# Hyena convolution spread between the query/key/value matmuls, attention spread between gate and projection tiles

## The chip, the cores and the metric

The kernel runs on one core of one Trainium2 chip. The metric is the device time of one execution in microseconds (us). All data are float32. In the trace a float32 matmul leaves two records, so a group "x128" is 64 matmuls; a transpose leaves one.

## The reference, cut to what matters

One trunk layer runs on 128 context tokens and 256 latent tokens (384 rows in all, width 2048).

```
mod  = silu(cond) @ w_ada + b_ada             # shift, scale, gate, twice
h    = rms_norm(x) * (1 + scale1) + shift1
proj = h @ w_in      # q 2048 | k 512 | v 512 | hyena 3 x 1024 | gate_attn 2048 | gate_hy 2048
y_attn = attention(rope(rms_norm(q)), rope(rms_norm(k)) + cache, v + cache) @ w_attn_o
u    = short_conv(hyena part) -> x0, x1, vh
y_hy = (x0 * long_conv(vh * x1, filter)) @ w_hy_o        # long_conv: product of spectra
m    = (sigmoid(gate_attn) * y_attn + sigmoid(gate_hy) * y_hy) @ w_out
x    = x + gate1 * rms_norm(m)
x    = x + gate2 * rms_norm(expert_choice_ffn(modulate(rms_norm(x))))     # 16 experts
```

There are 16 query heads and 4 key/value heads of width 128. The outputs are both streams and the context keys and values.

## The kernel before

Weights stream through `ring`, four slots of 2 MB. SyncE's queue loads them with `turn` (L262), four blocks a turn, each of 1024 rows by 512 columns (runs of 2 KB), and a block waits until the block four places ahead of it has been counted in `blocks_used` by TensorE. The order of all work is written out by hand for each engine; the engines meet at counting semaphores. The stages, with what TensorE runs in each:

- **Start** (to about 132 us): modulation columns (`ada`, L342, and `ada_cols`, L351), the Hyena filter and its spectrum.
- **Hyena projection**: six turns of `ada`, `channels` and `ada_cols`. `channels` (L365) computes four output tiles of 128 channels by 384 tokens in four PSUM banks, with the contraction outermost: all four tiles end together. ScalarE (L835) and VectorE (L1190) then empty the banks through the short convolution; the next turn's `channels` waits for each bank (`conv_free`).
- **Hyena long convolution**: transposes (`u_tokens`, L460), forward spectra (`u_spectrum`, L470 and L473), products of spectra on VectorE (L1219 to L1227), `inverse` (L486, L488), and VectorE's gating (L1233, L1236). Nothing else is interleaved.
- **Query, key, value**: six turns of `ada`, `tokens` (L376: three banks of 128 tokens by 512 columns, contraction outermost) and `ada_cols`. ScalarE empties the banks (L859), VectorE normalises and rotates (`qk_norm`, L1251 to L1277) with a power on GpSimd (L1017).
- **Attention**, one head after another, software-pipelined by two heads: `queries` (L540), `scores` (L547 to L549), VectorE's maxima (L1298 to L1302), ScalarE's exponentials (L885), VectorE's `normalise` (L1307, L1310), transposes of the probabilities (L557, L559), their copies (L893, L1316), and the product with the values (L567, L569), copied by ScalarE (L897). GpSimd stages queries and values (L1026, L1031).
- **Gates and projections**: 32 gate tiles (`channels` on `hT`, ScalarE's Sigmoid, L924 and L929), then the attention projection (16 tiles, `channels` on `oT`), whose tiles VectorE multiplies with the gate (L1337, L1343), then the Hyena projection (16 tiles of half the depth, L613; VectorE L1349 to L1351).
- **Output projection**: `tokens` for four blocks of 512 columns, with `broadcast_gates` (L625) in the first two. ScalarE squares and copies each bank (L938, L940), VectorE scales (L1382); then the norm and the residual.
- **Routing and experts** (from about 1641 us): expert weights stream in pieces of 1 MB (L311, L317).

Two lines set which tile ends when, in `channels` and in `tokens`:

```
for k in range(HK):
    for c in range(4):          # tokens: for m in range(MT)
```

Of the kernel before, what the change touches and what calls it, by code (L numbers as in the profile page):

```python
# [23 lines left out]
P = 128  # L24
# [47 lines left out]
def build(nc, x_prompt, x_sample, cache_k, cache_v, cols, w_ada, w_in, qk_g, w_attn_o, f1_w, f_vec, f2_w,  # L72
# [3 lines left out]
    with ctx:  # L76
# [23 lines left out]
        ring = view(ring_t, 0, 4, HK, NC_)  # L100
        pieces = view(ring_t, 0, 8, 2 * FF)
# [11 lines left out]
        rope_t = view(RA, 0, 2, 2, HD)  # L113
        rot = view(RA, 512, 2, 2, 2, HD)
        gain_b = view(RA, 1536, 2, HD)
        t_a, t_b = view(RA, 1792, NC_), view(RA, 2304, NC_)
        kT = view(RA, 0, NKV, T + PAST)
        q_st = view(RA, 2048, 2, MT, HD)
        qT = view(RA, 2816, 2, T)
        v_st = view(RA, 3584, 4, HD)  # L120
# [11 lines left out]
        oT = view(RC, 0, NH, T)  # L132
        mix = view(RC, 0, MT, D)
# [12 lines left out]
        qkN = view(RE, 0, MT, D + KVW)  # L146
        vN = view(RE, 7680, 4, KVW)
        kcN = view(RE, 9728, KVW)
        prob = view(RE, 10240, 2, 2 * 384 + TC)
        sg = view(RE, 0, 2 * KT, T)  # L150
# [6 lines left out]
        yhT = view(RF, 0, HYT, T)  # L157
# [9 lines left out]
        probT = view(RG, 1024, 896)  # L167
# [25 lines left out]
        U_BANK = ((4, 5, 0), (1, 2, 3))  # L193
        Z_BANK = ((4, 0, 2), (0, 2, 4))

        def bank(b, n=512, off=0, p0=0, p1=P):
# [4 lines left out]
        blocks_used = sem("blocks_used")  # L201

# [15 lines left out]
        q_staged, v_staged, at_trk, at_kT, at_trq, at_qT, at_s, at_max, at_exp, at_norm, at_trp, at_pa, at_pb, at_o, at_oc = (  # L218
            sem(n) for n in ("q_staged", "v_staged", "at_trk", "at_kT", "at_trq", "at_qT", "at_s", "at_max", "at_exp", "at_norm",
                             "at_trp", "at_pa", "at_pb", "at_o", "at_oc"))  # L220
        mod2_read, gate_sig, ao_done, ho_done, mod3_read = (
            sem(n) for n in ("mod2_read", "gate_sig", "ao_done", "ho_done", "mod3_read"))
# [17 lines left out]
        B_QKV = B_HY + 6  # L240
        B_GA = B_QKV + 6
        B_GB = B_GA + 4
        B_AO = B_GB + 2
        B_HO = B_AO + 2
        B_WO = B_HO + 1
        B_EX = B_WO + 2

        def block(w, h, c):

            return w[h * HK * P:(h + 1) * HK * P, ds(c * NC_, NC_)].rearrange("(k p) n -> p k n", p=P)  # L250

# [4 lines left out]
        def _(sp):  # L256
# [17 lines left out]
            for base, ada0, in0, n in ((B_HY, 8, 6, 6), (B_QKV, 14, 0, 6), (B_GA, 20, 12, 4)):  # L274
# [57 lines left out]
        def _(pe):  # L332
            mm, trp = nc.tensor.matmul, nc.tensor.transpose

            def ada(b, j0, rows_bank):


                for h in range(2):
# [1298 lines left out]
```

## Time and profile before

| What | us |
|---|---|
| Median of three runs (2710.15 to 2712.53) | 2712.01 |
| The profiled execution | 2710.64 |
| Its span, first to last instruction | 2708.8 |
| TensorE busy in the span | 2429.6 |
| VectorE, ScalarE, GpSimd busy | 508.5, 237.4, 56.0 |

The profiled execution is 1.8 us longer than its span. The views used are: the page (busy time of each engine, and the span in 40 equal slices of 67.7 us), busy time by stretch, the chain of work that ended last, the timeline of single instructions, the groups of instructions, and the DMA issues.

### The profile page before, as it was taken

The page shows a single profiled execution, that of the slowest core. Times are in us where ns is not written, and L with a number is a line of the kernel's source. Part 1 is how long each engine was busy: PE and PEld are TensorE (multiplying, and loading weights), DVE is VectorE, ACT ScalarE, POOL GpSimd, SP SyncE. Part 2 cuts the span into 40 slices and gives each one's busy share as a digit, 9 for nine tenths or more (in the row PEclk, how much of TensorE's full clock was granted, in tenths as well). Part 3 has the DMA queues.
Part 4 walks back from the last instruction along what each step waited for, and adds up shares of the span by engine and source line. Part 5 has one row for each costly group of instructions (what it writes and reads, how often), then busy time and mean ns, then how long its engine had stood idle before and what let it go on. Part 6 is the DMA issues. An engine that isn't in the chain of part 4 may idle for free.

```text
span 2708.8 us, 23285 instructions
## 1 busy us (share of the span) xinstructions
PE 2429.6 (90%) x9040; PEld 1126.0 (42%) x9040; DVE 508.5 (19%) x1008; ACT 237.4 (9%) x485; POOL 56.0 (2%) x74
## 2 busy tenths in 40 slices
PE   6899997999978999999999995988888888888886
PEld 2355554444455555555554442422222222222222
DVE  4200116112152000000011114311111112111125
ACT  1100000000052100000000002200000000000001
POOL 0000000000010000000000000010000000000000
PEclk8899999999999999999999997999999999999998
DMA  9954541545413542222222231499999999999994
GB/s 350 372 190 154 214 155 50 184 162 207 155 39 140 202 170 95 93 93 93 93 100 87 93 114 41 194 421 422 422 422 422 422 422 422 422 422 422 422 420 195
DMA packets 172048, 644.46 MB, mean 238 GB/s; under 512 B 8423, under 2 KB 8840, under 8 KB 122536
## 3 DMA queue, kind: packets, MB, share of 16 engines
q1 hardware_dynamic: 169736, 635.55, 59.7%
q10 hardware_dynamic: 2208, 8.24, 0.8%
q8 instruction: 27, 0.44, 0.1%
q0 software_dynamic: 64, 0.13, 0.0%
q14 instruction: 13, 0.11, 0.0%
HBM read 640.21 MB, written 3.67 MB: 238 GB/s over the span
## 4 chain that ended last, share of the span: by engine, by line
PE 65%; DMA 18%; issue 8%; DVE 5%; DVEq 2%; ACT 1%; SPq 1%; ACTq 0%; POOL 0%; POOLq 0%
PE PS L365 21%; DMA ring<-in_w_up 16%; PE PS L376 15%; PE PS L773 8%; PE PS L728 6%; PE PS L613 3%; PE PS L342 2%; PE PS L698 2%; DMA ring<-in_w_ada 2%; PE PS L673 1%; DVE RG L1480 1%; DMA ring<-in_w_in 1%; PE PS L421 1%; DVE RE L1310 1%; PE PS L625 1%
## 5 line engine op out<-in xcount | busy, mean ns | idle before, releaser
L365 PE MATMUL PS<-RB,ring 128*128 128x384 f32 x1792 | 585.5, 488 | 10.5 <-DVE RE L1190 4.4
L728 PE MATMUL PS<-ring,RF 128*48 128x512 f32 x1920 | 434.9, 595 | 87.4 <-DMA ring<-in_w_up 85.6
L365 PEld LDWEIGHTS PS<-RB,ring 128*128 128x128 f32 x1792 | 339.4, 190 | 259.2 <-issue 17.9
L728 PEld LDWEIGHTS PS<-ring,RF 128*48 128x48 f32 x1920 | 135.8, 123 | 382.1 <-issue 381.4
L1475 DVE TENSOR_TENSOR RC<-RC,PS 128x512 f32<-128x512 f32 x192 | 122.5, 683 | 740.9 <-PE PS L698 740.9
L376 PE MATMUL PS<-ring,RB 128*128 128x512 f32 x576 | 248.8, 593 | 0.0
L773 PE MATMUL PS<-ring,RF 128*48 128x512 f32 x960 | 225.2, 630 | 0.0
L365 PE MATMUL PS<-RC,ring 128*128 128x384 f32 x512 | 169.6, 494 | 8.7 <-DVE RE L1343 6.6
L376 PE MATMUL PS<-ring,RE 128*128 128x512 f32 x384 | 168.7, 601 | 5.7 <-DVE RE L1351 5.7
L376 PEld LDWEIGHTS PS<-ring,RB 128*128 128x128 f32 x576 | 108.9, 190 | 139.9 <-issue 139.9
L773 PEld LDWEIGHTS PS<-ring,RF 128*48 128x48 f32 x960 | 63.2, 130 | 165.9 <-issue 165.6
L365 PEld LDWEIGHTS PS<-RC,ring 128*128 128x128 f32 x512 | 98.6, 193 | 79.7 <-issue 8.8
L698 PE MATMUL PS<-RG,RF 48*128 48x512 f32 x384 | 114.9, 675 | 2.1 <-ACT RG L985 1.3
L376 PEld LDWEIGHTS PS<-ring,RE 128*128 128x128 f32 x384 | 74.0, 193 | 99.6 <-issue 93.3
L342 PE MATMUL PS<-ring,RG 128*32 128x512 f32 x768 | 93.9, 631 | 13.3 <-DMA ring<-in_w_ada 10.9
L613 PE MATMUL PS<-RF,ring 128*128 128x384 f32 x256 | 82.8, 486 | 2.2 <-DVE RE L1343 2.2
L1190 DVE SCALAR_TENSOR_TENSOR RE<-PS,KC,RE 128x127 f32 (+1 forms) x96 | 33.9, 410 | 256.0 <-ACT RE L835 251.7
L979 ACT ACTIVATE RF<-PS 48x512 f32<-48x512 f32 x32 | 18.9, 592 | 606.1 <-PE PS L728 553.4
L613 PEld LDWEIGHTS PS<-RF,ring 128*128 128x128 f32 x256 | 48.6, 190 | 36.4 <-DVE RE L1343 2.8
L985 ACT ACTIVATE RG<-PS 48x512 f32<-48x512 f32 x64 | 37.9, 593 | 274.0 <-PE PS L773 252.9
L698 PEld LDWEIGHTS PS<-RG,RF 48*128 48x128 f32 x384 | 33.6, 194 | 63.8 <-issue 57.9
L342 PEld LDWEIGHTS PS<-ring,RG 128*32 128x32 f32 x768 | 23.0, 113 | 69.0 <-issue 52.5
(213 smaller groups left out, 1175.5 us busy)
## 6 DMA issues: line engine op xcount, KB each, us to landing
ring<-in_w_gate SPq DMA_DIRECT2D x128, 1024.0 KB, 13.2
ring<-in_w_up SPq DMA_DIRECT2D x128, 1024.0 KB, 14.3
ring<-in_w_down SPq DMA_DIRECT2D x128, 1024.0 KB, 13.5
ring<-in_w_ada SPq DMA_DIRECT2D x48, 2048.0 KB, 14.2
ring<-in_w_in SPq DMA_DIRECT2D x40, 2048.0 KB, 7.8
ring<-in_w_attn_o SPq DMA_DIRECT2D x8, 2048.0 KB, 7.9
ring<-in_w_out SPq DMA_DIRECT2D x8, 2048.0 KB, 7.9
ring<-in_w_hy_o SPq DMA_DIRECT2D x4, 2048.0 KB, 8.0
```

The costliest lines, as they stand in the source:

```text
L342: last = mm(bank(rows_bank, p0=32 * g, p1=32 * g + 32), condS[:, kk, :], ring[:, j0 + h, k, :], start=kk < 4, stop=kk >= KT - 4)
L365: last = mm(bank(b0 + c, T), ring[:, j0 + h, k, c * P:(c + 1) * P], rhs[:, h * HK + k, :], start=(h == 0 and k == 0), stop=(h == 1 and k = ...
L376: last = mm(bank(b0 + m), lhs[:, h * HK + k, m * P:(m + 1) * P], ring[:, j0 + h, k, :], start=(h == 0 and k == 0), stop=(h == 1 and k == H ...
L421: mm(bank(n % 4), arg[0:HF, m * P:(m + 1) * P], f3[0:HF, c * NC_:(c + 1) * NC_], start=True, stop=True).then_inc(f_tapmm, 1)
L613: last = mm(bank(4 * (c % 2) + j, T), ring[:, c, k, j * P:(j + 1) * P], yhT[:, k, :], start=k == 0, stop=k == HYT - 1)
L625: mm(bank(b0 + n % 2), one, diag[:, n % 2, :], start=True, stop=True).then_inc(done, 1)
L698: mm(bank(4 + n % 4), s_cur[64 * u:64 * u + SLOTS, m * P:(m + 1) * P], ye[64 * u:64 * u + SLOTS, i, :], start=True, stop=True).then_inc(e_ ...
L728: last = mm(bank(n, p0=64 * u, p1=64 * u + SLOTS), xeT[:, kk, 0, :] if first else x_cur[:, kk, :], pieces[:, (2 * i + u) % 8, k * FF + n * ...
L773: last = mm(bank(2 + i, p0=64 * u, p1=64 * u + SLOTS), hTe[:, k, :], pieces[:, k, (2 * i + u) * NC_:(2 * i + u + 1) * NC_], start=k == 0, ...
L985: last = A(ye[64 * u:64 * u + SLOTS, i, :], bank(2 + i, p0=64 * u, p1=64 * u + SLOTS), ACT.Copy)
L1190: last = stt(out=hyT[:, ds(i * 4 + j, 1), a:b].rearrange("p o t -> p (o t)"), in0=bank(j, b - a, a + o), scalar=w, in1=hyT[:, ds(i * 4 + j ...
L1475: tt(facc[:, m, q], facc[:, m, q], bank(4 + n % 4), ALU.add).then_inc(e_acc, 1)
```

## The change

It does the following.

- **Order inside a block.** `channels` and `tokens` now run the contraction innermost, so that tiles end one after another; each has its own semaphore (`hy_tile`, `qkv_tile`, `wo_tile`) and is emptied while the next runs.
- **Hyena convolution.** `tokens` calls `beside_qkv` after each group of eight matmuls (36 such slots in the six turns). Slots 0 to 19 hold the Hyena work, slots 24 to 28 the transposes of the keys, slot 34 the first query. The order of the turns is key, value, then the four query blocks. The spectra use banks 3 and 4 for every product, the inverse bank 5.
- **Attention** runs one head per turn, between the 16 Hyena gate tiles and the 16 Hyena projection tiles. The two-head pipeline, the second query, score and probability buffers and GpSimd's staging go.
- **Gates.** A gate tile is 16 matmuls (`gate`), followed by its projection tile, and VectorE merges both at once (`merge`). Sigmoid becomes (1 + tanh(x/2))/2: ScalarE runs Tanh with scale 0.5, VectorE adds 1 and multiplies, and the factor 1/2 moves into the gains (`times` 0.5) and the mean square (0.25).
- **Weights.** Gate and attention projection blocks are now 2048 rows by 256 columns (`wide`, runs of 1 KB, 2 MB each); SyncE's loops are written out.
- **Small DMAs.** The rotary table and the query/key gains are loaded right after the filter's DFT table instead of after the Hyena products.

```diff
-                    for k in range(HK):
-                        for c in range(4):
-                            if free and h == 0 and k == 0:
-                                pe.wait_ge(conv_free, free(c))
+                    for c in range(4):
+                        if h == 0:
+                            pe.wait_ge(conv_free, i * 4 + (c + 1))
+                        for k in range(HK):
...
-            def tokens(b, j0, b0, lhs, then=None):
+            def tokens(n, b0, lhs, free, free_at, done, then):
...
+                    for m in range(MT):
+                        if h == 0:
+                            pe.wait_ge(free, free_at(m))
+                        for k in range(HK):
...
+                        then(h, m)
...
+            def beside_qkv(p):
...
+                elif p == 3:
+                    pe.wait_ge(u_cp, 3)
+                    u_spectrum(0, 0)
...
+                elif p == 5:
+                    pe.wait_ge(z_ready, 1)
+                    u_spectrum(0, 1)
...
+                elif p < 13:
+                    inverse(p - 9)
+                elif p < 16:
+                    pe.wait_ge(z_ready, p - 10)
+                    u_spectrum(1, p - 13)
+                elif p == 16:
+                    pe.wait_ge(z_ready, 6)
+                    inverse(4)
...
+            pe.wait_ge(qkv_raw, 18)
+            for t in range(KT):
+                n, j = N_GH + 3 * (t // 4), t % 4
+                if t > 0:
+                    attend(t - 1)
+                scores(t)
+                gate(n + j // 2, t)
+                probabilities(t)
+                if t < KT - 1:
+                    queries(t + 1)
+                block_in(n + 2)
+                if t > 0:
+                    pe.wait_ge(mixed, t)
+                for k in range(HYT):
+                    last = mm(bank(F1, T), ring[:, (n + 2) % 4, k, j * P:(j + 1) * P], hyT[:, k, :],
+                              start=k == 0, stop=k == HYT - 1)
+                last.then_inc(blocks_used if j == 3 else proj_tile, 1)
+            attend(NH - 1)
             pe.wait_ge(at_oc, NH)
+            for t in range(KT):
+                n, j = N_GA + 6 * (t // 4), t % 4
+                if j == 0:
+                    ada(0, n % 4, 7, n)
+                gate(n + 2 + j // 2 * 2, KT + t)
+                pa = n + 3 + j // 2 * 2
+                block_in(pa)
+                pe.wait_ge(mixed, KT + t)
+                for k in range(NH):
+                    last = mm(bank(F1, T), wide[:, pa % 4, k, j % 2 * P:(j % 2 + 1) * P],
...
+                if j == 3:
+                    ada_cols(20 + t // 4, 0)
+            pe.wait_ge(mixed, 2 * KT)
...
             act.dma_start(dft_t, dft).then_inc(dft_in, 16)
+            act.dma_start(rope_t[:, :, :, :], rope).then_inc(qk_in, 16)
...
+            for t in range(KT):
+                if t > 0:
+                    head_out(t - 1)
+                exponentials(t)
+                half_tanh(N_GH + 3 * (t // 4) + t % 4 // 2, t)
+                act.wait_ge(at_trp, t + 1)
+                A(probT[:, 0:512], bank(B_P[0]), ACT.Copy).then_inc(at_pa, 1)
+                if t < KT - 1:
+                    query_copy(t + 1)
...
+            product(0, 0)
+            product(0, 1)
+            dve.wait_ge(qk_in, 32)
+            gained_rope(1)
+            qk_norm(0, 0)
+            product(0, 2)
+            gained_rope(0)
+            for n in range(4):
+                hyena_out(n)
+            for j in range(3):
+                product(1, j)
+            for n in range(4, 8):
+                hyena_out(n)
+            qk_norm(1, 6)
+            qk_norm(2, 9)
+            qk_norm(3, 12)
...
+            for t in range(KT):
+                maxima(t)
+                normalise(t)
+                if t == 1:
+                    qk_squares(4, 15)
+                elif 2 <= t < 5:
+                    qk_rotate(4, t - 2)
+                if t == 4:
+                    qk_ready()
+                dve.wait_ge(at_trp, t + 1)
+                V.tensor_copy(probT[:, 512:896], bank(B_P[1], 384)).then_inc(at_pb, 1)
+                merge(t)
```

## Rows read from the trace of the kernel before

**Rows 1.** The page's 40 slices: busy tenths of TensorE and of the DMA engines.

```profile
PE   6899997999978999999999995988888888888886
...
DMA  9954541545413542222222231499999999999994
```

**Rows 2.** Stretches: length, PE, PEld, DVE, ACT, POOL busy, PEclk, DMA share, GB/s.

```profile
744.00:842.00 98.00, 74.55 (x406) 57.19 (x410) 53.66 (x150) 51.09 (x150) 11.92 (x20) 0.98 0.08 27
411.00:469.00 58.00, 41.71 (x162) 27.71 (x161) 40.44 (x69) 5.01 (x10) 0.00 (x0) 0.91 0.13 44
...
60.00:140.00 80.00, 69.02 (x342) 27.49 (x341) 23.69 (x48) 7.78 (x13) 0.00 (x0) 0.86 0.99 362
```

**Rows 3.** The chain that ended last, in order of time: start, us, what.

```profile
323.48 39.63 PE PS L365 x122
...
370.75 39.63 PE PS L365 x122
...
473.03 41.40 PE PS L376 x96
...
518.82 41.40 PE PS L376 x96
...
845.44 41.48 PE PS L365 x128
```

**Rows 4.** Timeline, Hyena convolution: start, us, engine, line, shape [idle before].

```profile
435.62 1.89 PE L488 MATMUL PS<-RC 128*128 128x256 f32 x8
...
437.79 1.89 PE L488 MATMUL PS<-RC 128*128 128x256 f32 x8
...
443.30 0.69 DVE L1219 TENSOR_TENSOR RC<-PS,RA 128x512 f32<-128x512 f32 x1
...
446.80 0.69 DVE L1227 TENSOR_TENSOR RC<-RC,RG 128x512 f32<-128x512 f32 x1
...
469.39 3.20 PE L342 MATMUL PS<-ring,RG 128*32 128x512 f32 x27 [1.60 <-DVE RF L1236]
```

**Rows 5.** Timeline, attention: key transposes, the first softmax, one head's period, the end.

```profile
745.16 1.94 PE L534 MATMUL PS<-KC,RE 128*128 128x128 f32 x16 [0.93 <-DVE SM L1288]
...
749.89 0.56 DVE L1298 TENSOR_REDUCE SM<-PS 128x1 f32<-128x384 f32 x1 [2.06 <-PE PS L549]
...
750.72 1.28 ACT L885 ACT_TABLE_LOAD   x1
...
755.20 1.52 PE L557 MATMUL PS<-KC,RE 128*128 128x128 f32 x6 [2.33 <-DVE RE L1310]
...
762.31 0.88 PE L557 MATMUL PS<-KC,RE 128*128 128x128 f32 x6 [1.10 <-DVE RE L1310]
...
767.72 0.88 PE L557 MATMUL PS<-KC,RE 128*128 128x128 f32 x6 [1.06 <-DVE RE L1310]
...
841.80 3.64 PE L342 MATMUL PS<-ring,RG 128*32 128x512 f32 x32 [0.78 <-ACT RC L897]
```

**Rows 6.** Timeline of PE: four gate tiles' blocks, and the output projection's first block.

```profile
1027.74 84.52 PE L365 MATMUL PS<-RB,ring 128*128 128x384 f32 x256 [2.36 <-ACT RE L924]
...
1465.92 23.88 PE L376 MATMUL PS<-ring,RE 128*128 128x512 f32 x48 [5.66 <-DVE RE L1351]
```

**Rows 7.** Timeline, end of the output projection: first ScalarE read, last VectorE product.

```profile
1640.91 0.60 ACT L938 ACTIVATE RF<-PS 128x512 f32<-128x512 f32 x1 [37.51 <-PE PS L376]
...
1644.63 0.69 DVE L1382 TENSOR_TENSOR RC<-RC,RB 128x512 f32<-128x512 f32 x1 [0.56 <-ACT RC L940]
```

**Rows 8.** Timeline of DVE: the first and the last instruction of one qk_norm.

```profile
561.09 0.69 DVE L1251 TENSOR_TENSOR RA<-RE 128x512 f32 x1 [30.71 <-ACT RE L859]
...
576.09 0.06 DVE L1277 MEMSET SM<- 128x1 f32 x1
```

**Rows 9.** DMA issues: tile, queue, operation, count, KB each, median us to landing.

```profile
ring<-in_w_in SPq DMA_DIRECT2D x40, 2048.0 KB, 7.8
```

**Rows 10.** Groups of ScalarE instructions: count | busy, mean ns | idle before.

```profile
L817 ACT ACT_TABLE_LOAD x4 | 5.1, 1283 | 1.5 <-issue 1.5
```

More of the change, by code:

```diff
@@ L543, in scores, with inverse @@
[L543 to L552 removed]
+            def inverse(n):
+                if n > 0:
+                    pe.wait_ge(yh_done, n)
+                cc = slice(n % 4 * P, (n % 4 + 1) * P)
+                for cs in range(2):
+                    mm(bank(5, TC), Z[:, 0, cs, cc], inv_c[:, cs, :], start=cs == 0, stop=cs == 1)
+                for q in range(4):
+                    last = mm(bank(5, TL, TC), Z[:, 1 + q // 2, q % 2, cc], inv_l[:, q // 2, q % 2, :],
+                              start=q == 0, stop=q == 3)
+                last.then_inc(z_inv, 1)
@@ new lines, in keys, with queries @@
+            def keys(g, b):
+                for m in range(4):
+                    src = kcN[:, g * HD:(g + 1) * HD] if m == 3 else kN[:, m, g * HD:(g + 1) * HD]
+                    last = trp(bank(b, P, m * P), src, ident)
+                last.then_inc(at_trk, 1)
+            def queries(h):
+                pe.wait_ge(qk_done, 2 + h // 4)
+                if h > 0:
+                    pe.wait_ge(at_qT, h)
+                for m in range(MT):
+                    last = trp(bank(B_Q, P, m * P), qN[h // 4][:, h % 4, m, :], ident)
+                last.then_inc(at_trq, 1)
@@ L617, in _, with gate @@
-            pe.wait_ge(ho_done, 16)
+            def gate(n, t):
+                block_in(n)
+                if t > 0:
+                    pe.wait_ge(gate_read, t)
+                for k in range(KT):
+                    last = mm(bank(F0, T), wide[:, n % 4, k, t % 2 * P:(t % 2 + 1) * P], hT[:, k, :],
+                              start=k == 0, stop=k == KT - 1)
+                last.then_inc(blocks_used if t % 2 else gate_tile, 1)
+            pe.wait_ge(qkv_raw, 18)
[15 more added lines that the diff above has]
+                last.then_inc(blocks_used if j == 3 else proj_tile, 1)
@@ L837, in _, with u_copy @@
                       scale=col[:, ds(i * 4 + (C_CW + 24 + j), 1)]).then_inc(conv_mid, 1)
[L839 removed]
+            def u_copy(n, b):
+                half, m = n // MT, n % MT
                 act.wait_ge(u_tr, n + 1)
[L841 to L846 removed]
@@ L912, in _ @@
+            head_out(NH - 1)
             act.wait_ge(at_oc, NH)
@@ L1239, in _ @@
-            dve.wait_ge(qk_in, 32)
-            for a in range(2):
+                dve.wait_ge(u_dft, 3 * half + j + 1)
+                if half and j == 0:
+                    dve.wait_ge(z_inv, 4)
+                hc, hsn = spec[:, j, 0, hs], spec[:, j, 1, hs]
+                uc, us = bank(3), bank(4)
+                dve.drain()
+                tt(Z[:, j, 0, :], uc, hc, ALU.mult)
+                tt(tmp, us, hsn, ALU.mult)
+                tt(Z[:, j, 1, :], uc, hsn, ALU.mult)
+                dve.drain()
```

694 lines of the change are left out of this document (325 added, 369 removed).

## The prediction

> **What bounds the kernel now.** I began with the slices: TensorE is at nine tenths almost everywhere from the third slice to the 24th, with dents at slices 7 (407 to 474 us), 12 and 13 (745 to 880 us) and 25 (1626 to 1693 us). From slice 27 on it is the DMA engines that are full [rows 1]. So up to 1641 us TensorE's own work is the limit, the experts behind it are limited by weight traffic, and the routing between them is not touched. Then the stretches of the dents: in the 58 us of the Hyena convolution TensorE is busy 41.7 us, in the 98 us of attention 74.6 us, and the DMA engines are at 0.13 and 0.08 [rows 2]. Nothing there is missing but TensorE work that could fill the holes, which is what the change moves in. The chain and the timelines give the durations of single pieces, which I use as prices.
>
> Everything after the output projection starts from its end, so what is won before is won in the whole. The sum is made against the profiled execution, 2710.64 us; the median of the runs shown is 1.4 us above it.
>
> **The prices of TensorE.** 64 matmuls of 384 columns take 41.48 us, 0.648 each; 48 of 512 columns take 41.40 us, 0.863 each; the period of a turn of `tokens` is 45.79 us, so `ada` with `ada_cols` costs 4.39 us [rows 3]. 16 transposes take 1.94 us, 0.121 each [rows 5]. Contraction innermost puts matmuls back to back into one bank: `inverse` does this already, with four matmuls of 256 columns and two of 128 in 2.17 us [rows 4]; at 0.43 each the four take 1.73 us. So the new order costs nothing for itself.
>
> **1. Hyena projection.** Turns start 47.27 us apart (323.48 to 370.75), the work is 41.48 + 4.39 = 45.87 [rows 3]: 1.4 us of waiting for banks that were emptied only after all four tiles ended. Now tiles 0 to 2 end up to 15.6 us (24 matmuls) before the turn does and the fourth bank is needed 15.6 us into the next. Five boundaries: **-7.0**.
>
> **2. Hyena convolution.** The last matmul of the projection ends at 370.75 + 39.63 = 410.38, the next `ada` starts at 469.39 [rows 3, 4]; less 0.8 for `ada_cols`, 58.2 us. The work stays on TensorE: 24 transposes 2.9, 20 spectrum matmuls of 512 columns 17.3, eight inverses 17.4, together 37.6. Gain 20.6; by the busy time of the stretch instead (41.7 us, part of it at a low clock, 0.91 on average [rows 2]) it would be 16.5. I take 20.6, as the work now stands between matmuls at full clock. The cover: a slot is eight matmuls of 512 columns, 6.9 us. A product of spectra takes VectorE 4.2 us (443.30 to 446.80 + 0.69) [rows 4]. The tightest slots are 14, 15 and 16: a spectrum, the product, and 6.9 us later the next wait, some 2.4 us to spare. The product of slot 7 is queued on VectorE behind `qk_norm` of the keys, which takes 15.1 us [rows 8]; it starts as turn 0 ends, and the product is needed at slot 9, some 36 us later. The other `qk_norm` start behind the Hyena work and have a turn of over 45 us each. If this cover fails, the stall comes back at slots 14 to 16.
>
> **3. Attention.** From 744.23 (745.16 less 0.93 idle) to 841.80: 97.6 us. One head's period is 5.41 us (762.31 to 767.72) with 1.06 idle, so 4.35 us of work [rows 5]. 16 heads are 69.6, the keys 1.9: 71.5 us. Gain **26.1**; by busy time (74.6) 23.0. I take the period, since gaps between semaphores are inside it. The cover is the gate tile, 16 matmuls or 10.4 us. From the end of the first head's scores to the first probability transpose pass 749.69 to 755.20, 5.5 us, and that includes most of a table load of 1.28 us [rows 5]. VectorE also carries the last `qk_norm` at turns 1 to 4, in parts of up to 5 us behind `normalise`: 5.5 + 5 is about the gate tile, and the probabilities' copy behind it is needed only after the 5.2 us of the projection tile. The values are multiplied one turn later. GpSimd's staging copies go and nobody waited for them.
>
> ScalarE now mixes Exp, Tanh and Copy. Before, the Copy behind the Sigmoids reloaded the table in each of four turns, 1.28 us each [rows 10]. If every switch loaded, one such load would fall into the chain (6.8 us) and the others beside the gate and projection tiles: nothing on TensorE, and the bound stays. The Trainium skill (ScalarE: Activation LUTs, Table sets) says that Exp and Tanh share a set and that cheap functions such as Copy are in every set, with 2.7 us for a switch to another set. The first part this trace cannot show; the second it contradicts, as those four loads stand before a Copy. By the page the loads vanish, and the sum is the same.
>
> **4. Gates to output projection.** From 841.80 to 1640.91: 799.1 us [rows 5, 7]. The work: 512 gate, 256 attention and 128 Hyena matmuls, 896 x 0.648 = 580.7 (also today); four `ada` with columns 17.6; 192 output matmuls 165.6; eight broadcasts 6.9. Together 770.8, so 28.3 us are waits and lower clock: a wait of 2.36 us ahead of a block of 84.5 us where 83.0 is the work, one of 5.66 us ahead of a block that took 23.9 instead of 20.7 [rows 6]. Each tile's gate is now read 5.2 to 10.4 us before its bank is needed, so these go. What is new: TensorE waits for the last head's copy (0.8, as at 841.80 now [rows 5]), and for the last merge (5.66 for four tiles now, so 1.4 for one), with perhaps one clock dip as above (1.5). 774.5 us; gain **24.6**.
>
> **5. End of the output projection.** ScalarE and VectorE need 3.7 us after the last matmul for three tiles [rows 7]; two of them now end earlier: **-2.5**.
>
> **6. What it adds.** The rotary table (2 KB by 128 partitions) and the gains (1 KB) now load while the DMA engines are full, 0.99 at 362 GB/s [rows 2]: 0.39 MB, up to +1.1 us, taken in full. The wait for the last value of `qkv_raw` before attention: one copy, +0.7. ScalarE's queue issues them ahead of a copy of modulation rows that is not late.
>
> **DMA.** Gate and attention projection blocks come as runs of 1 KB instead of 2 KB. A 2 MB block lands in 7.8 us [rows 9]. If time went with the number of runs alone it would be 15.6 us; if with bytes alone 7.8. The shortest cover is at the first attention gate tile: the slot is free when the last Hyena gate tile ends, then 0.9 + 5.2 + 1.9 + 0.8 + 3.6 = 12.4 us; inside the next stage it is 10.4 + 0.8 + 3.6 = 14.8 us. So 0 to 6 us; I take 0, since a block may take half as long again as now, 12 us, and still be on time, and the DMA engines are at two tenths there [rows 1]. The Trainium skill (DMA: Bandwidth & Descriptors, Why small descriptors are slow) gives a fixed three cycles a packet beside one per 32 bytes; by that 1 KB runs cost 4 to 5% more, an estimate of 8.2 us, and the sum stays too.
>
> **Sum.** 7.0 + 20.6 + 26.1 + 24.6 + 2.5 - 1.8 = 79.0 us; 2710.6 - 79.0 = 2631.6, and 1.4 more to stand against the median: **2633 us**.
>
> **The rivals.**
> *A wait in every head stays.* TensorE's queue is in order, so whatever is late in softmax stops the gate work too, and only one head is in flight instead of two. For it: 1.06 us idle per head today, 16 x 1.1 = 18 us back, **2651 us**. Against: 5.5 us of chain under 10.4. 0.10.
> *The Hyena slots do not hide.* Only 2.4 us to spare at slots 14 to 16, one bank pair for all products, VectorE shared with `qk_norm`. At most the whole of part 2 returns, **2654 us**. Against: one product at a time fits. 0.06.
> *Slower.* The same in-order queue, with the softmax chain longer than the gate tile by 79/16 = 4.9 us, so of more than 15.3 us: that is the point from which it decides. It would need every switch of table to fall into the chain (three loads, 3.8 us), and VectorE's normalisation parts in it (5 us), in all heads: 14.3 + 2 for merges, 5.9 us over, 94 us back, **2727 us**. VectorE's parts occur in four heads only. 0.03.
> *The change does part of what it says*, with the clock falling at many short waits: some 10 to 30 us lost in all, in the range. 0.04.
>
> **How the numbers follow.** The forecast has 0.77. Its own bounds: no waits or dips at all, 2627; the busy-time bounds of parts 2 and 3 (+7.2) and late blocks (+6), 2646. The first two rivals reach 2651 and 2654, and both in part together some more; the range is **2622 to 2660**. A measurement here tells about 0.2% (5 us) from no change. Faster by more than that 0.96, within 0.01, slower 0.03.
>
> **What would show it.** The routing should begin near 1562 us. TensorE should be at nine tenths from 130 us to there, with the Hyena operations standing in the turns of `tokens` and those turns at 45.8 us plus the slots' work, 318 us in six. Head turns should be 10.4 + 5.2 + 4.35 = 19.9 us apart, attention gate tiles 20.7 us. Wrong would be: idle time of TensorE before the probability transposes or the spectra, DMA as the releaser of a gate tile, or a granted clock well below 1 in these stages.

## The result, and the profile after

| What | before, us | after, us |
|---|---|---|
| Median of four runs each | 2712.27 (2710.15 to 2716.46) | 2620.57 (2620.07 to 2625.91) |
| Profiled execution | 2710.64 | 2621.07 |
| Its span | 2708.8 | 2619.3 |
| TensorE busy | 2429.6 | 2410.7 |

The ratio of the two is 0.9666, with a 95% interval of 0.9650 to 0.9682: the change takes 91.7 us off. The forecast was 2633 us with a range of 2622 to 2660. The direction, the place and the mechanism were right; the size was 12.4 us too small, and the time lies 1.4 us below the range.

The page of after, TensorE's and the DMA engines' busy tenths and the granted clock in 40 slices (of 65.5 us now):

```profile
PE   5899999999999999999999977988888888888886
...
PEclk8999999999999999999999998999999999999998
DMA  9964553444412223454433220899999999999995
```

The dents of before [rows 1] are gone from TensorE's row: it stays at nine tenths from slice 3 to slice 23, and the full DMA engines that mark the experts' weight streams begin in slice 26 (0.8), from 1637 us on, not in slice 27. The stretches of the same stages (length, PE, PEld, DVE, ACT and POOL busy, clock, DMA share, GB/s) answer to [rows 2]:

```profile
407.00:722.00 315.00, 314.97 (x1004) 149.52 (x1002) 83.83 (x157) 20.99 (x36) 9.09 (x4) 1.00 0.46 164
722.00:1036.00 314.00, 313.60 (x1149) 199.79 (x1149) 70.09 (x188) 57.36 (x161) 2.27 (x1) 1.00 0.24 81
1036.00:1386.00 350.00, 348.96 (x1184) 202.29 (x1184) 17.70 (x32) 10.68 (x21) 0.00 (x0) 1.00 0.46 153
```

Query, key and value with the Hyena convolution in them, attention with the Hyena gates, and the attention gates: TensorE is busy in 977.5 of 979 us, at a granted clock of 1.00, the upper of its two levels (2.4 GHz). So nothing was left to gain here but the matmuls themselves. This is what it still waited for from 130 to 1640 us (the waits: who for whom, us in all, times, longest). The first two lines already belong to the routing, and the next two, both waits for DMA, stand ahead of the first block of the Hyena projection, at 125.5 and 132.3 us. What is left between 134.5 and 1558 us is 1.7 us:

```profile
PE PS L707 <- DVE RC L1484: 17.1, 1, 17.1
PE PS L728 <- DVE RG L1524: 8.4, 1, 8.4
PE PS L366 <- DMA ring<-in_w_ada: 3.5, 1, 3.5
...
PE PS L392 <- DMA ring<-in_w_in: 2.1, 1, 2.1
...
PE PS L407 <- DVE RC L1417: 0.6, 1, 0.6
...
PE PS L366 <- ACT RE L984: 0.6, 1, 0.6
PE PS L605 <- ACT RA L929: 0.3, 1, 0.3
PE PS L675 <- DMA ring<-in_w_attn_o: 0.2, 1, 0.2
```

Stage by stage in the two profiled executions (the sums of the forecast are regrouped by stage; the key transposes and the first query, 2.3 us, moved from attention to the stage before):

| Stage | before | after | gain | forecast |
|---|---|---|---|---|
| Start to the end of the Hyena projection | 410.38 | 407.09 | 3.3 | 5.9 |
| Query, key, value with the convolution | 333.85 | 314.89 | 19.0 | 18.3 |
| Attention to the last output matmul | 896.65 | 836.19 | 60.5 | 52.3 |
| From there to GpSimd's power | 4.85 | 2.33 | 2.5 | 2.5 |
| The power to the end of the span | 1063.1 | 1058.8 | 4.3 | 0 |

The five gains are 89.6 us against 79.0.

### The profile page after: what moved, and what is told of

The parts are those of the page before. It is cut to its first block, busy times and chain, and to the rows that moved or that the text cites. A ratio compares the mean times of both kernels' runs of the same rounds, so it can differ in the third digit from the quotient of the medians.

```text
span 2619.3 us, 22817 instructions
## 1 busy us (share of the span) xinstructions
PE 2410.7 (92%) x9040; PEld 1120.4 (43%) x9040; DVE 508.1 (19%) x1025; ACT 234.5 (9%) x478; POOL 44.2 (2%) x54
## 4 chain that ended last, share of the span: by engine, by line
PE 75%; DMA 19%; DVE 2%; ACT 1%; issue 1%; SPq 1%; DVEq 1%; POOL 0%; ACTq 0%; POOLq 0%
PE PS L407 16%; DMA ring<-in_w_up 16%; PE PS L640 12%; PE PS L392 10%; PE PS L840 9%; PE PS L675 6%; PE PS L795 6%; PE PS L659 3%; PE PS L366 3%; DMA ring<-in_w_ada 2%; PE PS L765 2%; PE PS L740 1%; DVE RG L1566 1%; DMA ring<-in_w_in 1%; PE PS L630 1%
## 5 line engine op out<-in xcount | busy, mean ns | idle before, releaser
L795 PE MATMUL PS<-ring,RF 128*48 128x512 f32 x1920 | 435.7, 596 | 79.2 <-DMA ring<-in_w_up 77.2
L840 PE MATMUL PS<-ring,RF 128*48 128x512 f32 x960 | 231.9, 645 | 0.0
L407 PE MATMUL PS<-ring,RC 128*128 128x512 f32 x384 | 165.7, 592 | 0.6 <-DVE RC L1417 0.6
L407 PEld LDWEIGHTS PS<-ring,RB 128*128 128x128 f32 x576 | 108.1, 190 | 132.1 <-issue 131.8
L675 PE MATMUL PS<-RE,ring 128*128 128x384 f32 x384 | 126.5, 486 | 0.0
L407 PEld LDWEIGHTS PS<-ring,RC 128*128 128x128 f32 x384 | 72.9, 190 | 92.0 <-issue 91.4
L675 PEld LDWEIGHTS PS<-RE,ring 128*128 128x128 f32 x384 | 73.0, 190 | 50.9
L659 PE MATMUL PS<-RE,ring 128*128 128x384 f32 x256 | 85.2, 486 | 0.0
## 6 DMA issues: line engine op xcount, KB each, us to landing
ring<-in_w_attn_o SPq DMA_DIRECT2D x8, 2048.0 KB, 15.8
```

The source lines that it names most:

```text
L407: last = mm(bank(b0 + m), lhs[:, h * HK + k, m * P:(m + 1) * P], ring[:, (n + h) % 4, k, :], start=(h == 0 and k == 0), stop=(h == 1 and k ...
L659: last = mm(bank(F1, T), ring[:, (n + 2) % 4, k, j * P:(j + 1) * P], hyT[:, k, :], start=k == 0, stop=k == HYT - 1)
L675: last = mm(bank(F1, T), wide[:, pa % 4, k, j % 2 * P:(j % 2 + 1) * P], qN[k // 4][:, k % 4, :, :].rearrange("p m d -> p (m d)"), start=k ...
L795: last = mm(bank(n, p0=64 * u, p1=64 * u + SLOTS), xeT[:, kk, 0, :] if first else x_cur[:, kk, :], pieces[:, (2 * i + u) % 8, k * FF + n * ...
L840: last = mm(bank(2 + i, p0=64 * u, p1=64 * u + SLOTS), hTe[:, k, :], pieces[:, k, (2 * i + u) * NC_:(2 * i + u + 1) * NC_], start=k == 0, ...
```

## The experiments

All are edits of the kernel after, except the last two. Each profile is compared with the repeat of after, which is the first experiment, where the text doesn't say otherwise. "The power" is the start of GpSimd's first instruction behind the output projection, 1558.58 us in the repeat.

**1. The same kernel again.** No edit.

> The changed kernel once more, unedited. The chain of the changed kernel gives 82.7 us won up to the end of the output projection (1640.9 to 1558.2), and 6.8 us more behind it, of which the forecast had 2.5. Theory A: the rest, some 4 us, is chance, the phase in which TensorE's clock falls in the last expert (granted clock 0.75, 0.91, 0.83 in three stretches of it before, 0.83, 1.0, 1.0 after), so the time of single executions spreads over 2618 to 2626 us, and the profile's stretch from the end of the output projection to the last instruction lies anywhere in 1060 to 1068 us while the stretch up to it stays within 2 us of 1558. Theory B (rival): the change shortened the end lastingly; then all times lie within 2 us of 2620 and the stretch behind the projection is 1061 again.

Measured: 2619.77 us median (2618.86 to 2625.28), ratio 0.9666 (0.9648 to 0.9683), span 2617.1 us. The output projection ends at 1556.27 us, 1.9 earlier than in the first profile; TensorE's first projection matmul had come 1.8 earlier (132.69 against 134.46). The times spread as theory A said, over 6.4 us; but from the end of the output projection to the end of the span it is 1060.8 us again (1061.1 in the first profile), as theory B said. One repeat doesn't settle it, and experiments 10 and 11 take it up. A result that lies 2 us or less from another says nothing about an edit here.

**2. The small DMAs at their old place.**

```diff
             act.dma_start(dft_t, dft).then_inc(dft_in, 16)
-            act.dma_start(rope_t[:, :, :, :], rope).then_inc(qk_in, 16)
-            act.dma_start(gain_b, qk_g.rearrange("(o a) d -> o (a d)", o=1).to_broadcast([P, 2 * HD])
...
                 rows(i * 4 + 4, 5, tmp)
+            act.dma_start(rope_t[:, :, :, :], rope).then_inc(qk_in, 16)
+            act.dma_start(gain_b, qk_g.rearrange("(o a) d -> o (a d)", o=1).to_broadcast([P, 2 * HD])
```

> The rotary table and the gains are loaded behind the last modulation rows of the start instead of behind the DFT table. In the changed kernel the first Hyena projection matmul starts at 134.46 us instead of 132.35, and its block of 128 records takes 43.24 us instead of 41.5 at a clock of 0.96. Theory A: both come from these 0.39 MB in a start that is limited by DMA; the block starts near 132.4 us and the time is 2 to 4 us lower, 2617 us. Theory B (rival): the start differs from one execution to the next by as much; no difference beyond 1 us, and the block starts between 132 and 135 us in either kernel.

Measured: 2623.07 us (2619.17 to 2624.66), ratio 0.9667 (0.965 to 0.9685). The first turn begins at 134.92 us, not earlier than with the DMAs early (132.1 to 135.3 in the nine other profiles of the new code). So nothing here says that they set the start. The other half of theory A fails too: the first block of the Hyena projection doesn't get faster. It is slow wherever the new code runs, and only there:

```profile
132.35 41.54 PE L365 MATMUL PS<-RB,ring 128*128 128x384 f32 x128 [1.86 <-DMA ring<-in_w_in]
```

```profile
134.46 43.24 PE L392 MATMUL PS<-RB,ring 128*128 128x384 f32 x128 [2.13 <-DMA ring<-in_w_in]
```

These are before and after. All three profiles of before show 41.54 us, all ten of the new code 43.2 to 44.5, this run 44.48. From 132 to 140 us the granted clock is 1.00 in before and 0.79 in after. Why the clock comes back later isn't shown; just ahead of it TensorE waits 2.9 to 5.2 us for a block of `w_ada` in the new code and 1.0 to 1.2 us in before.

**3 and 4. A longer softmax chain.** Six, then twelve more maxima on VectorE in every head, of the same tile and into a spare column; the result is the same.

```diff
             for t in range(KT):
                 maxima(t)
+                for _ in range(6):          # 12 in the other run
+                    V.reduce_max(SM[:, 123:124], bank(B_S[0], 384), AX_X)
+                    dve.drain()
                 normalise(t)
```

> VectorE does six more maxima (each with a drain, some 0.64 us) in every head between the scores and the exponentials, 3.8 us more in the chain from scores to probabilities. In the changed kernel that chain ends at 787.2 us and the gate tile at 792.7, 5.4 us to spare. Theory A (the gate tile covers the chain, and only what sticks out costs): no change, within 1 us of the changed kernel, except up to 4 us in heads 1 to 4, where the last normalisation sits behind it. Theory B (rival: VectorE's time in the head turn is itself on the path, by its place in the in-order queue before the copy and the merge): 16 x 3.8 = 61 us more.

> The same with twelve more maxima, 7.7 us a head. Theory A: 2.3 us stick out behind the gate tile in every head, 16 x 2.3 = 37 us, and up to 25 us more where TensorE's clock falls behind these waits: 2657 to 2685 us; TensorE's idle time before the probability transposes is 2.3 us a head. Theory B: 123 us more, 2744 us.

Measured: with six 2623.92 us (2619.92 to 2626.97), ratio 0.967; the output projection ends at 1558.61 us, 2.3 later than in the repeat, but the first turn had begun 2.6 later (135.32 us), and no wait for the probabilities appears. With twelve 2658.03 us (2654.57 to 2661.97), ratio 0.9805. Its waits, and one head in its timeline:

```profile
PE PS L617 <- DVE RA L1398: 27.7, 16, 2.0
```

```profile
788.42 10.48 PE L640 MATMUL PS<-RB,ring 128*128 128x384 f32 x32
788.62 7.51 DVE L1384 TENSOR_REDUCE SM<-PS 128x1 f32<-128x384 f32 x12 [2.41 <-PE PS L607]
...
800.60 0.88 PE L617 MATMUL PS<-KC,RA 128*128 128x128 f32 x6 [1.70 <-DVE RA L1398]
```

Twelve maxima are 7.6 us, and TensorE waits 1.7 of it (2.0 at most): the cover of the softmax chain is 5.6 to 5.9 us, as the profile of after says (below). Six, 3.8 us, fit in it. The expected 37 us look met, since the span grows by 35.6 us, but in part by luck: 1.8 us are a later start (134.46 us) and 1.3 stand behind the power. The heads themselves are 21.52 us apart (788.42 to 809.94) instead of 19.60, 1.9 us each where 2.3 were expected, and the attention ends 32.9 us later than in after, which has the same start (1069.37 against 1036.48). Of these 27.7 are the waits as the profile counts them. This is the mechanism of the first rival (a wait in every head) and of the "slower" one: it needs a chain longer than the gate tile's 10.3 us, and the real one is about 4.5.

**5. The Hyena convolution in one piece.** All twenty slots run ahead of the query/key/value turns, and ScalarE's and VectorE's orders follow.

```diff
+            for p in range(20):
+                beside_qkv(p)
...
-                       qkv_tile, lambda h, m: beside_qkv(6 * i + 3 * h + m))
+                       qkv_tile, lambda h, m: beside_qkv(6 * i + 3 * h + m) if 6 * i + 3 * h + m >= 20 else None)
```

> The slots 0 to 19 of the Hyena convolution are all run before the query/key/value turns, and VectorE's and ScalarE's parts with them; all else is as in the changed kernel. Theory A (the gain of this part is TensorE's idle time, and the price of the work does not depend on its place): the stretch between the last Hyena projection matmul and the first ada of the next stage is some 77 us: per half three products of 4.3 us with one bank pair, each waiting for its spectrum (1.7, 3.4, 3.4), and four inverses of 2.2 with VectorE's 1.4 between them, 37 us a half. Of this 37.6 us is work that the changed kernel has too, so the time is 40 us longer, 2660 us, up to 8 more where the clock falls. Theory B (rival): in the changed kernel the slots also delay the emptying of the query/key/value banks, so that taking them out wins some of it back; less than 25 us more, and the turns of tokens without slots shorter than the changed kernel's turn less its slots' work.

Measured: 2671.62 us (2667.17 to 2675.27), ratio 0.9849 (0.9828 to 0.9869), span 2666.5, the power at 1606.63 (+48.1). Theory A expected 2660 us, up to 2668 with a lower clock. The miss upwards has its reason in the timeline of TensorE:

```profile
417.30 3.70 PE L504 MATMUL PS<-RE,RC 128*128 128x512 f32 x8 [3.91 <-DVE RC L1279]
420.84 0.60 PE L493 MATMUL PS<-KC,RE 128*128 128x128 f32 x4
425.35 5.40 PE L504 MATMUL PS<-RE,RC 128*128 128x512 f32 x8 [3.91 <-DVE RC L1279]
...
435.18 0.68 PE L513 MATMUL PS<-RC 128*128 128x128 f32 x4 [4.00 <-DVE RC L1279]
...
491.43 3.64 PE L366 MATMUL PS<-ring,RG 128*32 128x512 f32 x32
```

The stage takes 407.75 to 491.43, 83.7 us, where the kernel before needed 58.2: the change had also cut the banks of the spectra to one pair. TensorE waits about 4 us for each of VectorE's products, 24.8 us in all, and 8.4 us for VectorE's gating, and at the low clock that follows (mean 0.89 from 408 to 471 us) the same four matmuls (eight records) take 5.4 instead of 3.7 us. 83.7 less the 37.6 us of work is 46.1; with a start that was 1.8 us later that is nearly the 48.1. The stage took 6.7 us more than the 77 expected. The thrift with banks is free only while something else fills the wait.

**6. Attention in one piece.** The sixteen heads run first, then the sixteen gate and projection tiles.

```diff
             for t in range(KT):
-                n, j = N_GH + 3 * (t // 4), t % 4
                 if t > 0:
                     attend(t - 1)
                 scores(t)
-                gate(n + j // 2, t)
                 probabilities(t)
                 if t < KT - 1:
                     queries(t + 1)
+            attend(NH - 1)
+            for t in range(KT):
+                n, j = N_GH + 3 * (t // 4), t % 4
+                gate(n + j // 2, t)
...
-            attend(NH - 1)
             pe.wait_ge(at_oc, NH)
```

ScalarE's and VectorE's orders follow here too.

> All 16 heads run before the 16 Hyena gate and projection tiles, with the changed kernel's single buffers; no work is added. Theory A (the tiles cover the softmax chain and are the whole gain): between scores and probability transposes TensorE waits 4.6 us a head, and 0.5 us for the copy of the transposed probabilities, so a head takes 9.3 us instead of 4.1 within a turn: 16 x 5.2 = 83 us more, 2703 us, and up to 50 us more where TensorE's clock falls behind the waits. That would be slower in this stage than the kernel before, whose heads took 5.4 us. Theory B (rival: the gain comes from what was dropped, the staging copies on GpSimd and the second buffers): at most 30 us more, 2650 us.

Measured: 2742.56 us (2740.33 to 2744.56), ratio 1.011 (1.0093 to 1.0127): slower than the kernel before. Attention now lasts from 721.84 to 908.90 us, 187.1 us for 16 heads. The stretch and two heads of TensorE's timeline:

```profile
722.00:897.00 175.00, 101.10 (x360) 75.34 (x360) 57.58 (x162) 47.82 (x135) 2.27 (x1) 0.75 0.04 12
```

```profile
728.02 0.87 PE L617 MATMUL PS<-KC,RA 128*128 128x128 f32 x6 [4.43 <-DVE RA L1397]
...
738.74 1.13 PE L617 MATMUL PS<-KC,RA 128*128 128x128 f32 x6 [4.43 <-DVE RA L1397]
...
744.09 0.77 PE L628 MATMUL PS<-RA,RE 128*128 128x128 f32 x2 [3.37 <-issue]
744.65 2.77 PE L630 MATMUL PS<-RA,RE 128*128 128x256 f32 x6
```

With one head in flight each waits 4.4 us for its softmax, 70.8 us in all; with the waits for copies TensorE is idle 79.0 of the 187.1 us. It is busy for the other 108.0 us with work that takes 65.9 in after (16 times 4.12, below), as the granted clock falls to 0.75 on average: the same three matmuls of L630 (six records) take up to 2.77 us instead of 1.46. The stage is 121 us longer than its work, where theory A had 83 us and up to 50 more for the clock. The kernel before paid for its attention in buffers and GpSimd's staging, and got 5.41 us a head for it [rows 5], 6.0 on average over the stage; this one has given those up and takes 11.7 us a head on average without its cover. The interleaving is therefore worth 122.2 us (the power at 1680.73 against 1558.58) to the new code and, by the forecast of part 3, 26.1 us to the old.

**7. The old order of the contraction.** In the Hyena and in the output projection, with a semaphore for each tile kept.

```diff
-                    for c in range(4):
-                        if h == 0:
-                            pe.wait_ge(conv_free, i * 4 + (c + 1))
-                        for k in range(HK):
+                    for k in range(HK):
+                        for c in range(4):
+                            if h == 0 and k == 0:
+                                pe.wait_ge(conv_free, i * 4 + (c + 1))
...
+                            if h == 1 and c < 3 and k == HK - 1:
+                                last.then_inc(hy_tile, 1)
```

> The contraction is outermost again in the Hyena projection's channels and in the output projection's blocks, so that the tiles of a block end together; the query/key/value blocks stay as changed. Theory A: the wait of 1.4 us at each of five boundaries comes back (turns 47.3 us apart instead of 45.88), the stretch from the last output matmul to the first residual norm on GpSimd grows from 2.3 to 4.8 us, and the start of the first query/key/value turn waits little: 9.5 us more in all, 2630 us. Theory B (rival: matmuls of one bank in a row cost or save something themselves): the work of a block of 64 matmuls differs from 41.48 us by more than 0.3 us.

Measured: 2623.03 us (2618.78 to 2630.28), ratio 0.9676 (0.9656 to 0.9695), span 2617.0. The return of the 1.4 us a turn that theory A expected didn't come. The timeline shows why, around one end of a turn:

```profile
219.56 2.60 ACT L919 ACTIVATE RE<-PS,KC 128x384 f32 x4 [39.14 <-PE PS L392]
...
221.07 0.99 PE L375 MATMUL PS<-KC,RG 128*128 128x2 f32 x8
...
222.00 3.64 PE L366 MATMUL PS<-ring,RG 128*32 128x512 f32 x32
...
225.57 4.78 PE L392 MATMUL PS<-RB,ring 128*128 128x384 f32 x14
```

ScalarE begins three matmuls before the block ends, and the `ada` work between the turns is enough for VectorE to free the banks. Turns stay 45.88 us apart (179.69 to 225.57), and a block of 64 matmuls takes 41.55 us in this order as in that of after, so theory B fails as well. From the last matmul to the power it is 3.1 us.

**8. The old order with one signal for all tiles.** As 7, and ScalarE waits for the whole block.

```diff
-                    if j < 3:
-                        act.wait_ge(hy_tile, i * 3 + (j + 1))
-                    else:
-                        act.wait_ge(blocks_used, i * 4 + (4 * B_HY + 4))
+                    act.wait_ge(blocks_used, i * 4 + (4 * B_HY + 4))
```

(and the same in the output projection)

> The run before with the contraction outermost again in the Hyena and output projections hardly lost time (2623.0 us against 2620.6): there each tile still had its own semaphore, raised by its last matmul, so tile 0 was signalled three matmuls before the block ended, and the banks came free before the next turn needed them. Here the same order has one signal for all tiles, as in the kernel before. Theory A (it is the signal that costs, not the order of the contraction): the turns of the Hyena projection are 47.3 us apart instead of 45.9 (five boundaries, +7.0), TensorE waits about 1.4 us for VectorE's convolution at each, the end of the output projection to GpSimd's power is 4.8 us instead of 3.3 (+1.5), and the output projection starts later by these 7 us alone: 2617.0 + 8.5 = about 2626 us for a profiled execution, 2631 us at most by the medians. Theory B (the turns were shortened by something else, by the shorter instruction sequence of ScalarE or by the small DMAs that went): turns stay 45.9 us apart and the time stays within 2 us of 2623.

Measured: 2629.75 us (2628.64 to 2630.87), ratio 0.9698 (0.9681 to 0.9715), span 2627.0.

```profile
180.00 1.56 PE L392 MATMUL PS<-RB,ring 128*128 128x384 f32 x4
181.83 0.91 PE L392 MATMUL PS<-RB,ring 128*128 128x384 f32 x2 [0.27 <-DVE RE L1253]
183.41 39.61 PE L392 MATMUL PS<-RB,ring 128*128 128x384 f32 x122 [0.67 <-DVE RE L1253]
...
230.69 4.78 PE L392 MATMUL PS<-RB,ring 128*128 128x384 f32 x14 [0.67 <-DVE RE L1253]
```

Turns are 47.28 us apart again (183.41 to 230.69), the waits for the convolution are back, and from the last output matmul to the power it is 4.8 us (1562.84 to 1567.66). The power is 9.0 us later than in experiment 7 with the same start, where 8.5 were expected. So of the 9.5 us of parts 1 and 5 of the prediction, 7.0 and 1.7 come from the signal of each tile and at most 0.8 (the 3.1 of experiment 7 against 2.33) from the order of the matmuls: theory A holds.

**9. Sigmoid's table instead of Tanh's.** ScalarE computes a sigmoid of half the argument in place of the hyperbolic tangent; the rest is as in after.

```diff
-                A(sig[t % 2], bank(F0, T), ACT.Tanh, scale=0.5).then_inc(gate_read, 1)
+                A(sig[t % 2], bank(F0, T), ACT.Sigmoid, scale=0.5).then_inc(gate_read, 1)
```

> ScalarE runs Sigmoid instead of Tanh, still with scale 0.5, in all 32 gate tiles: the gates are computed otherwise than in the reference, with the same instructions around them. The changed kernel shows three table loads in all, so Exp, Tanh and Copy share a table. Theory A (the cover of the chain also takes table loads): two loads of 1.28 us a head, ScalarE 41 us busier, the chain from scores to probabilities 1.3 us longer at most and still 4 us inside the gate tile: no change beyond 2 us, 2621 us. Theory B (rival: loads on ScalarE delay the copies that TensorE waits for): 16 x 1.3 to 16 x 2.6 us, 20 to 40 us more.

Measured: 2621.21 us (2618.91 to 2624.99), ratio 0.9665 (0.9649 to 0.9681), span 2617.1. The table loads in its groups of instructions:

```profile
L977 ACT ACT_TABLE_LOAD x16 | 20.5, 1283 | 0.3
L993 ACT ACT_TABLE_LOAD x16 | 20.5, 1283 | 2.1
```

ScalarE is busy 40.9 us longer (275.4 against 234.5) and the time is the same. In a head the load ahead of the exponentials runs while ScalarE waits for the scores and their maxima, the one ahead of the sigmoid under the gate tile. The Tanh form of the change saves loads, and that buys nothing here.

**10 and 11. The kernel before, again, twice.**

> The kernel before, unchanged, profiled a second time. Behind the power that closes the output projection the profiled execution of before needs 1063.1 us to the end of its span, that of after 1058.8 and its repeat 1058.5. Theory A (the 4.3 us are chance: which clock TensorE is granted in the last two experts, 61.7 us or 58.7 us between the last two experts' silus): this execution or the next one shows 58 to 60 us for it and a rest of 1059 to 1060 us, and all up to the output projection is within 2 us of the first profile. Theory B (the change itself shortens the rest, by what it leaves the stage behind): both show 61.7 us and 1063 us again.

> The kernel before, unchanged, a third profile, for the same question: by theory A at least one of the two repeats has a rest of 1059 to 1060 us behind the power of the output projection, by theory B both have 1063.

Measured: single times of 2707.68 and 2715.36 us, spans 2705.9 and 2713.6. Behind the power they take 1060.3 and 1063.0 us. In the first, the last expert's ScalarE instructions are 58.7 us apart, in the second 61.7, as in the first profile of before:

```profile
2595.79 0.59 ACT L979 ACTIVATE RF<-PS 48x512 f32<-48x512 f32 x1 [3.42 <-DVE RG L1480]
2654.45 0.59 ACT L979 ACTIVATE RF<-PS 48x512 f32<-48x512 f32 x1 [38.63 <-PE PS L728]
```

```profile
2598.74 0.59 ACT L979 ACTIVATE RF<-PS 48x512 f32<-48x512 f32 x1 [3.42 <-DVE RG L1480]
2660.48 0.59 ACT L979 ACTIVATE RF<-PS 48x512 f32<-48x512 f32 x1 [40.21 <-PE PS L728]
```

Both lengths occur with the new code too: 58.65 in after and its repeat, 61.99 in experiment 3. So the same program can end either way, and most of the last line of the stage table can be chance: 1.5 us remain between 1060.3 and 1058.8. It isn't settled, though. The short end came in nine of ten profiles of the new code (1057.8 to 1059.9 us behind the power; 1064.3 in the tenth) and in one of three of before. Whether the change makes it more frequent stays open. The start scatters as well: TensorE's first projection matmul comes at 132.35, 131.98 and 137.15 us in three profiles of before, and between 132.1 and 135.3 in those of the new code. (The first of the two repeats of before is within 2 us of the first profile up to the power, the second 4.8 us later, by its start.)

## Why the prediction was right in its mechanism and wrong in its size

In the profiled executions the gain was 10.6 us more than the forecast: 8.2 in attention, gates and output projection (parts 3 and 4), 4.3 behind the output projection, 0.7 in the stage of query, key and value, less 2.6 at the start. The rest of the 12.4 us lies between profile and median: 1.4 had been added to the sum for it, and the median of after lies 0.5 below its profiled execution. The steps that failed are the prices of TensorE's work and waits in parts 3 and 4, and the zero behind the output projection; had either been right, the time would have lain in the range.

**Part 1 (7.0): right in size, half right in cause.** Turns are 45.88 us apart (319.73 to 365.61). The step says that the tiles now end up to 15.6 us early; experiments 7 and 8 show that 1.9 us of head start, from a semaphore on each tile, does the same.

**Part 2 (20.6): right.** The stage took 314.1 us (407.92 to 721.98), with not one wait in it. The prediction's own terms, six turns of 45.79, 37.6 and the 2.3 that moved in, make 314.6; its "318 us in six" doesn't follow from them. The value from pieces between full-clock matmuls was the right choice over the busy time (16.5). Experiment 5 shows the same work at 83.7 us when nothing covers it.

**Parts 3 and 4 (26.1 and 24.6): the step that failed, by its prices.** The mechanism is as forecast. One head of after:

```profile
763.10 10.48 PE L640 MATMUL PS<-RB,ring 128*128 128x384 f32 x32
...
764.80 0.58 ACT L977 ACTIVATE RA<-PS,SM 128x384 f32<-128x384 f32 x1 [2.52 <-DVE SM L1387]
...
766.69 0.94 DVE L1395 TENSOR_SCALAR RA<-RA,SM 128x384 f32<-128x384 f32 x3
...
773.42 0.82 PE L617 MATMUL PS<-KC,RA 128*128 128x128 f32 x6
...
774.51 5.33 PE L659 MATMUL PS<-RE,ring 128*128 128x384 f32 x16
...
779.67 0.38 PE L628 MATMUL PS<-RA,RE 128*128 128x128 f32 x2
...
782.70 10.48 PE L640 MATMUL PS<-RB,ring 128*128 128x384 f32 x32
```

The probabilities are ready at 767.6 us and needed at 773.4: 5.8 us of cover, in heads without a part of `qk_norm`. The turn is 19.60 us where 19.9 was forecast. They gained 8.2 us more, by three terms that were too large. A head's attention work is 1.09 + 3.03 = 4.12 us (773.42 to 774.51, 779.67 to 782.70), not 4.35: 16 times 0.23 are **3.7 us**. I had taken a period less its idle time from [rows 5]; the idle time of such a row counts only from the modelled end of the matmul before it, which lies 0.16 us behind the point where the next may start (10.48 against a period of 10.32 above), and the first transposes after a wait are slower (0.88 against 0.82). Second, 16 matmuls take 10.32 us, 0.645 each, not 0.648: the 41.48 us of [rows 3] include a slower start behind `ada` (in after the first 16 matmuls of such a block take 10.43 us) and part of that tail. Over 896 matmuls that is **2.8 us**. Third, the waits: 0.6 us at the last merge where 1.4 were taken, no dip of the clock (1.5), 0.6 for the last head's copy (0.8), 0.3 for the last value of `qkv_raw` (0.7), and 0.2 for a weight block that had no term: **2.7 us**. These are 9.2 us. About 0.8 goes the other way: `ada` with its columns, and the slower start behind it, take 4.6 us here instead of 4.39, four times.

**Part 5 (2.5): right**, 4.85 to 2.33 us, 1.7 of it by the signals.

**Part 6 (-1.8): wrong in its cause.** The start was later by 2.1 us, but experiments 1, 2, 10 and 11 show that it moves without the change. The first block was slower by 1.7, and that does come with the new code, in ten profiles of ten (experiment 2). It isn't the small DMAs that the 1.1 us were for, as it stays with these late; the prediction had no term for it, and its cause is open. Of the 0.7 us for `qkv_raw` 0.3 came.

**DMA (0): right.** Wide blocks of `w_in` land in a median of 8.2 us against 7.8 [rows 9]. The Trainium skill (DMA: Bandwidth & Descriptors, Why small descriptors are slow) led to an estimate of 8.2 us, and the trace agrees. The blocks of the attention projection are another matter: they land in a median of 15.8 us. The first two (16.4 and 23.2 us) share the engines with 3 MB of residual inputs from ScalarE's queue and with a block between them. Three later ones take 15.7 to 17.0 us with no such inputs beside them: each is the third block that SyncE issues within 5 us (1123.37, 1126.09 and 1127.80, for one). The other three land in 8.2 to 8.4. The first attention gate tile had 11.6 us of cover (issued at 1028.49, needed at 1040.05), near the 12.4 that I had worked out, and its block was in time. The attention projection's first block, which I had not worked out, had 16.2 us (from 1034.41), and TensorE waited once:

```profile
1050.84 2.85 PE L675 MATMUL PS<-RF,ring 128*128 128x384 f32 x8 [0.20 <-DMA ring<-in_w_attn_o]
```

My step did not name this: I had counted the size of the packets, not what else is under way.

**ScalarE's tables (0): right.** After holds three table loads in all, and Exp, Tanh and Copy alternate without one. The Trainium skill (ScalarE: Activation LUTs, Table sets) says so; experiment 9 shows that it didn't matter. The four loads that stand before a Copy in the kernel before [rows 10] stay unexplained.

**Behind the output projection (0): 4.3 us**, a term that I had put at nothing and not into the range either. The runs show the end of one program in two lengths 3 us apart (experiments 10 and 11); that all of the 4.3 us is chance is not shown. My lower bound, 2627 us for no waits at all, was built from the same two prices as the forecast, so it could not cover an error in them; the 5 us beneath it were a margin without a term.

**The rivals.** A wait in every head: none of it (cover 5.8 us). The Hyena slots: none of it. Many short waits with a falling clock: none of it, the clock is 1.00 in all three stages. Slower: it needs 4.9 us over the gate tile, and twelve added maxima, 7.6 us, lengthen the span by 35.6 us and still leave the kernel at 0.9805.

## What to carry to other kernels

When a stall is to be filled, count the gain as the stage's length less the work at the durations it has between full-clock matmuls, and take these from the distance between two starts in an unbroken row, not from busy time or a period less its idle: small errors add up over hundreds of pieces (here 3.7 us in 16 heads and 2.8 us in 896 matmuls). Give the lower bound its own error in the prices and the scatter of repeated profiles. Before a loop nest is turned to make tiles end early, try a semaphore on each tile's last matmul: here that alone gave 8.7 of 9.5 us.

## What the runs showed of the hardware

- Short waits cost more than their own length, through the granted clock: in experiment 6 TensorE was idle 79.0 us of 187.1, and its work, 65.9 us at the upper level (2.4 GHz), took 108.0 at a mean granted clock of 0.75, with three matmuls at up to 2.77 us instead of 1.46. In experiment 4 sixteen waits of 1.7 to 2.0 us, 27.7 in all, cost 32.9.
- The last expert has two lengths, 58.7 and 61.7 us, in the same program.
- Thirty-two more table loads, 1283 ns each, cost nothing where each lies under a wait of ScalarE.
- An issue of one block of 2048 runs takes SyncE 0.37 us as a rule, but 10.3 us at 1040.18 in after, with 3 MB from ScalarE's queue and two blocks of its own just issued, and 3.6 to 4.1 us at 1127.80, 1214.96 and 1302.12, where it is the third block within 5 us and ScalarE had issued nothing.
- When three loads of 2 MB are issued within 5 us, the second lands in 11.5 to 13.0 us and the third in 15.7 to 17.0, where one alone takes 7.8 to 8.2.
- The order of the contraction changes nothing in the rate: 64 matmuls of 384 columns take 41.55 us either way (experiment 7).
